# A gate table spread by one-hot products: one comparison for both keys of eight tokens, and one multiplication by the gates

## The chip, the cores and the metric

The kernel runs on one core of a Trainium2 chip. The metric is the time of one execution on the device in microseconds (us). Engines are named as in the profile: PE is TensorE (PEld its weight loads), DVE is VectorE, ACT is ScalarE, POOL is GpSimd, SP is SyncE, which here only issues transfers.

## The reference

One decoder layer over 1024 tokens of width 1024: two kinds of attention, an output projection, and a mixture of 16384 single-neuron experts that are addressed by product keys. The change lies in the mixture:

```python
vals, idx = lax.top_k(sc, PEER_TOPK)          # per token and head: the best 16 of 128 keys, twice
cand = vals[:, :, 0, :, None] + vals[:, :, 1, None, :]
best, flat = lax.top_k(cand.reshape(..., 256), PEER_TOPK)
i1 = jnp.take_along_axis(idx[:, :, 0], flat // PEER_TOPK, axis=-1)
i2 = jnp.take_along_axis(idx[:, :, 1], flat % PEER_TOPK, axis=-1)
expert = i1 * PEER_NKEYS + i2                 # 8 heads x 16 = 128 experts for each token
gate = jax.nn.softmax(best, axis=-1)
act = jax.nn.gelu(jnp.einsum('td,thkd->thk', tc, u_emb[expert]))
out = jnp.einsum('thk,thkd->td', act * gate, v_emb[expert])
```

## The kernel before

The kernel is a sequence of stages on one core: projections, two attentions, the output projection, `route` (which finds 128 experts and gates for each token), `spread_gates`, and `run_experts`. The first 384 tokens (SPT = 3 tiles of 128) get their experts by gathering rows. For the other 640 tokens (NDT = 5 tiles, TD = 640) the kernel computes with all 16384 experts, and needs the gate of each token and expert in a dense table, which is zero where an expert wasn't chosen. `spread_gates` makes this table and writes it to `core.scr_g` in device memory, from where `run_experts` reads it.

`route` leaves `slotT` in SBUF, f32: for slot s (on the partitions, 128 of them) and token t it holds the first key, the second key and the gate. In `spread_gates` the view `flat` has these as planes 0, 1 and 2. A token's 128x128 table is a product of two factors with the slots as the summed dimension: `first[s, i]` is the gate if the first key is i, else 0; `second[s, j]` is 1 if the second key is j, else 0.

The work goes in octets of 8 tokens (OCT = 8, NOCT = 80 octets, 16 octets to a tile), with two buffers (BUFS = 2) for the factors and four pairs of PSUM banks (PS_BUFS = 4). Each engine runs its own loop, ordered by semaphores:

- DVE (L1676 to L1686) compares a bf16 iota with the second keys of the octet (L1676, 1024 elements for each partition, written as [key, token] to `one2`), then makes `first` in 8 operations, one for each token (L1683: iota equal to the first key, times the gate, f32), and then converts the last 2 of the octet's 8 second factors to f32 and turns them from [key, token] to [token, key] order (L1686). It waits on `second_act`, `second_dve` and `spread_done` for free buffers, and on `ones_ready` in front of L1686.
- ACT (L1708) converts and turns the other 6 (ON_ACT = 6) second factors (`widen`), and copies each finished octet from PSUM to `gates` in SBUF (L1716, `copy_out`). The order is widen(n+1), copy_out(n).
- PE (L1699) waits for all three parts and for a free pair of banks, and does one f32 product for each token, `first[:, b, t, :]` as the stationary operand (weights) and `second[:, b, t, :]` as the moving one. The profile counts two weight loads and two matmuls for one such product, so 16 of each for an octet.
- SP (L1652) sends each finished tile of `gates` (8 MB) to device memory; near the end it loads what the next stage needs first (L1655 to L1658), and after the last octet it sends the last tile in two parts (L1662).

In the trace `one` is the tile `one2`, `iota_g` is `iota_f`, `iota_gb` the bf16 `iota`, and `slot_keys` is `keysT`.

Of the kernel before, what the change touches and what calls it, by code (L numbers as in the profile page):

```python
# [6 lines left out]
P = 128  # L7
# [22 lines left out]
PH, NKEY, PQ, TOPK = 8, 128, 256, 16  # L30
# [8 lines left out]
TD = SEQ - T0  # L39
# [18 lines left out]
bf16 = mybir.dt.bfloat16  # L58
i32 = mybir.dt.int32
u32 = mybir.dt.uint32  # L60
ALU = mybir.AluOpType
# [39 lines left out]
def clear_counts(nc, sems):  # L101

    with nc.Block() as block:
        @block.sync
        def _(sp):
            for s in sems:
                sp.sem_clear(s)
# [1494 lines left out]
def spread_gates(core, slotT, outer, hn_in, u_in, last_sent):  # L1602

    nc, ps = core.nc, core.ps
    OCT = 8
    TU = BANK // NKEY
    NB = OCT // TU
    BUFS = 2
    PS_BUFS = 4
    PER_TILE = P // OCT  # L1610
    NOCT = TD // OCT
    ON_ACT = 6
    LEAD = 8
    with ExitStack() as ctx:
        sb, new_sem = core.scope(ctx)
        made = []

        def sem(name):
            made.append(new_sem(name))
            return made[-1]  # L1620

        with nc.sbuf_tensor("gates1", [P, NKEY, P], f32, side="right") as gates1:
            pass
        lead = Lead(core, outer)
        gates = [ctx.enter_context(nc.sbuf_tensor("gates0", [P, NKEY, P], f32, side="right")), gates1]
        one2 = sb("one2", [P, BUFS, NKEY, OCT], bf16)
        first = sb("first", [P, BUFS, OCT, NKEY])
        second = sb("second", [P, BUFS, OCT, NKEY])
        iota_f = sb("iota_g", [P, NKEY])
        iota = sb("iota_gb", [P, NKEY, OCT], bf16)  # L1630
        keysT = sb("slot_keys", [P, TD], bf16)
        iota_in = sem("iota_in_g")
        iota_ready, keys_ready = sem("iota_ready_g"), sem("keys_ready_g")
        ones_ready, first_ready, second_act, second_dve = (sem(x) for x in (
            "ones_ready", "first_ready", "second_act", "second_dve"))
        spread_done, gates_out = sem("spread_done"), sem("gates_out")
        sent = [sem(f"gates_sent{k}") for k in range(2)]
        clear_counts(nc, (*made, hn_in, *u_in, *last_sent))
        block = ctx.enter_context(nc.Block())
        flat = slotT[:, :, :, :].rearrange("p z i t -> p z (i t)")  # L1640

        def need(eng, sem_, value):
            if value > 0:
                eng.wait_ge(sem_, value)

        @block.sync
        def _(sp):
            sp.dma_start(iota_f[:, :], core.i["c_iota"]).then_inc(iota_in, 16)
            dst = core.scr_g.rearrange("j i t -> i j t")
            for tile in range(NDT - 1):  # L1650
                sp.wait_ge(gates_out, (tile + 1) * PER_TILE)
                sp.dma_start(dst[:, :, tile * P:(tile + 1) * P], gates[tile % 2][:, :, :]).then_inc(sent[tile % 2], 16)  # L1652
            assert NDT % 2 == 1
            sp.wait_ge(sent[1], 16 * (NDT // 2))
            sp.dma_start(lead.u_raw[:, 0, :], core.i["uT"][0]).then_inc(u_in[0], 16)  # L1655
            sp.dma_start(lead.hn_hi[:, :, :].bitcast(f32), core.scr_hi).then_inc(hn_in, 16)
            sp.dma_start(lead.hn_lo[:, :, :].bitcast(f32), core.scr_lo).then_inc(hn_in, 16)
            sp.dma_start(lead.u_raw[:, 1, :], core.i["uT"][1]).then_inc(u_in[1], 16)  # L1658
            sp.wait_ge(sent[0], 16 * (NDT // 2))
            sp.wait_ge(gates_out, NDT * PER_TILE)  # L1660
            for part, js in enumerate((slice(0, LEAD), slice(LEAD, NKEY))):
                sp.dma_start(dst[:, js, (NDT - 1) * P:], gates[0][:, js, :]).then_inc(last_sent[part], 16)  # L1662

        @block.vector
        def _(dve):
            dve.wait_ge(iota_in, 16)
            nc.vector.tensor_copy(iota[:, :, :], iota_f[:, :].rearrange("p (i o) -> p i o", o=1)
                                  .to_broadcast([P, NKEY, OCT])).then_inc(iota_ready, 1)
            nc.vector.tensor_copy(keysT[:, :], flat[:, 1, :]).then_inc(keys_ready, 1)
            dve.wait_ge(iota_ready, 1)  # L1670
            dve.wait_ge(keys_ready, 1)
            for n in range(NOCT):
                b = n % BUFS
                need(dve, second_act, n - BUFS + 1)
                need(dve, second_dve, n - BUFS + 1)
                nc.vector.tensor_tensor(  # L1676
                    one2[:, b, :, :], iota[:, :, :],
                    keysT[:, n * OCT:(n + 1) * OCT].rearrange("p (o t) -> p o t", o=1)
                    .to_broadcast([P, NKEY, OCT]), ALU.is_equal).then_inc(ones_ready, 1)
                need(dve, spread_done, n - BUFS + 1)  # L1680
                for t in range(OCT):
                    at = n * OCT + t
                    nc.vector.tensor_scalar(first[:, b, t, :], iota_f[:, :], flat[:, 0, at:at + 1], flat[:, 2, at:at + 1],  # L1683
                                            ALU.is_equal, ALU.mult).then_inc(first_ready, 1)
                dve.wait_ge(ones_ready, n + 1)
                nc.vector.tensor_copy(second[:, b, ON_ACT:, :], one2[:, b, :, ON_ACT:].rearrange("p i t -> p t i")  # L1686
                                      ).then_inc(second_dve, 1)

        @block.tensor
        def _(pe):  # L1690
            for n in range(NOCT):
                b, bank = n % BUFS, NB * (n % PS_BUFS)
                pe.wait_ge(first_ready, (n + 1) * OCT)
                pe.wait_ge(second_act, n + 1)
                pe.wait_ge(second_dve, n + 1)
                need(pe, gates_out, n - PS_BUFS + 1)
                for t in range(OCT):
                    slot = ps[:, bank + t // TU, :].rearrange("p (i t) -> p t i", t=TU)[:, t % TU, :]
                    last = nc.tensor.matmul(slot, first[:, b, t, :], second[:, b, t, :], start=True, stop=True)  # L1699
                last.then_inc(spread_done, 1)  # L1700

        @block.scalar
        def _(act):
            def widen(n):
                b = n % BUFS
                act.wait_ge(ones_ready, n + 1)
                need(act, spread_done, n - BUFS + 1)
                nc.scalar.activation(second[:, b, 0:ON_ACT, :], one2[:, b, :, 0:ON_ACT].rearrange("p i t -> p t i"),  # L1708
                                     ACT.Copy).then_inc(second_act, 1)

            def copy_out(n):
                tile, q, bank = n // PER_TILE, n % PER_TILE, NB * (n % PS_BUFS)
                if q == 0:
                    need(act, sent[tile % 2], 16 * (tile // 2))
                act.wait_ge(spread_done, n + 1)
                nc.scalar.activation(  # L1716
                    gates[tile % 2][:, :, q * OCT:(q + 1) * OCT].rearrange("p j (u t) -> p j u t", u=NB),
                    ps[:, bank:bank + NB, :].rearrange("p u (j t) -> p j u t", t=TU), ACT.Copy).then_inc(gates_out, 1)

            widen(0)  # L1720
            for n in range(NOCT):
                if n + 1 < NOCT:
                    widen(n + 1)
                copy_out(n)
    return lead
# [608 lines left out]
```

## Time and profile before

| what | value |
|---|---|
| median of 3 runs | 3493.8 us (3491.78 to 3494.56) |
| the profiled execution | 3491.57 us, of which the span of the trace is 3489.8 us |
| mean granted PE clock | 0.966 of 2.4 GHz |
| stage of the change (`spread_gates`) | about 1299 to 1540 us of the span |

A row of the grouped views reads: line, engine, operation, tile written and tiles read, shape (partitions x elements for each partition), count, then busy time and the mean duration of one in ns, and then the idle time of the engine just before these instructions and what ended it. In the timeline the first number is the start in us and the second the time from the start of the first to the end of the last instruction of the row. Instructions of one engine overlap a little, so the distance between two starts is less than a duration.

### The profile page before, as it was taken

How to read it: one execution, taken by the hardware profiler on the slowest of the kernel's cores; microseconds unless marked ns; L12 is line 12 of the kernel's file. 1: busy time of each engine (PE TensorE's matmuls, PEld its weight loads, DVE VectorE, ACT ScalarE, POOL GpSimd, SP SyncE). 2: the span in 40 equal slices, each digit the busy share in tenths (PEclk: the TensorE clock that was granted, in tenths of full speed). 3: DMA queues.
4: the chain of work that ended last, by engine and by line, in shares of the span. 5: the costliest groups of instructions: out<-in, count | busy, mean ns of one | idle time of the engine just before them, and what ended most of it. 6: DMA issues, size and time to landing. Idle time of an engine off the chain costs nothing.

```text
span 3489.8 us, 48281 instructions
## 1 busy us (share of the span) xinstructions
PE 3149.8 (90%) x17341; PEld 2488.5 (71%) x17341; DVE 2190.4 (63%) x5408; ACT 1066.5 (31%) x1515; POOL 980.6 (28%) x943
## 2 busy tenths in 40 slices
PE   8997888997999936659999999999999999999997
PEld 4445666744887826658889877887788888788885
DVE  2112333323598979967888877777677777544544
ACT  2224545511333319962222222222122222222221
POOL 0000000000122220003333356566566656322222
PEclk9998889998999969999999999999999999999998
DMA  5213102112111103688777789999999999765765
GB/s 192 81 64 108 30 6 49 24 43 80 67 63 61 53 5 97 193 265 290 258 259 256 253 323 363 359 378 370 344 373 382 364 359 376 263 248 218 255 232 197
DMA packets 319597, 715.63 MB, mean 205 GB/s; under 512 B 48816, under 2 KB 154544, under 8 KB 318000
## 3 DMA queue, kind: packets, MB, share of 16 engines
q0 software_dynamic: 110592, 402.70, 31.4%
q1 hardware_dynamic: 201792, 299.95, 24.6%
q10 hardware_dynamic: 7024, 10.51, 0.8%
q8 instruction: 112, 1.84, 0.2%
q14 instruction: 77, 0.63, 0.1%
HBM read 633.91 MB, written 75.50 MB: 203 GB/s over the span
## 4 chain that ended last, share of the span: by engine, by line
PE 50%; DVE 3%; DMA 2%; issue 1%; ACT 0%; POOL 0%; POOLq 0%; ACTq 0%; DVEq 0%
PE psum L1965 23%; PE psum L1949 22%; PE psum L1992 5%; DMA w<-scr_g 1%; DVE res L2139 1%; DVE res L2128 1%; DMA res<-u_rows,eid 0%; DVE u_lo L2096 0%; DMA rows<-scr_rows 0%; DVE w_lo L2113 0%; DMA v_ring<-v_rows,eidT 0%; POOL v_ring L1933 0%; DVE v_lo L2118 0%; ACT u_hi L2027 0%; DVE w L2104 0%
## 5 line engine op out<-in xcount | busy, mean ns | idle before, releaser
L1933 POOL DMA_INDIRECT v_ring<-v_rows,eidT x384 | 443.2, 1154 | 622.3 <-PE psum L1992 513.8
L1949 PE MATMUL psum<-hn_hi_e,u_hi 128*128 128x320 f32 x1792 | 557.7, 311 | 27.4 <-DVE w L2108 18.9
L1949 PE MATMUL psum<-hn_lo_e,u_hi 128*128 128x320 f32 x1792 | 557.0, 311 | 0.0
L1949 PE MATMUL psum<-hn_hi_e,u_lo 128*128 128x320 f32 x1792 | 556.1, 310 | 0.0
L1965 PE MATMUL psum<-v_hi,w_hi 128*128 128x512 f32 x1280 | 511.5, 400 | 21.7 <-DVE res L2128 11.0
L2128 DVE TENSOR_TENSOR res<-psum,res 128x512 f32<-128x512 f32 x640 | 431.9, 686 | 122.8 <-PE psum L1965 122.4
L1965 PE MATMUL psum<-v_hi,w_lo 128*128 128x512 f32 x1280 | 501.0, 391 | 0.0
L1965 PE MATMUL psum<-v_lo,w_hi 128*128 128x512 f32 x1280 | 500.9, 391 | 0.0
L1926 POOL DMA_INDIRECT res<-u_rows,eid x288 | 337.7, 1173 | 336.8 <-DVE dots L2139 277.7
L2139 DVE CUSTOM_DVE_ANT_0 res<-res,rows 128x1024 f32<-128x1024 f32 x288 | 349.4, 1218 | 56.4 <-DMA res<-u_rows,eid 45.8
L2033 ACT ACTIVATE psum<-psum 128x640 f32<-128x640 f32 x112 | 77.1, 688 | 938.5 <-PE psum L1949 938.5
L1949 PEld LDWEIGHTS psum<-hn_hi_e,u_hi 128*128 128x128 f32 x1792 | 339.4, 189 | 32.4 <-issue 28.0
L1965 PEld LDWEIGHTS psum<-v_hi,w_hi 128*128 128x128 f32 x1280 | 241.1, 188 | 148.4 <-issue 78.3
L1949 PEld LDWEIGHTS psum<-hn_lo_e,u_hi 128*128 128x128 f32 x1792 | 339.3, 189 | 4.5
L1949 PEld LDWEIGHTS psum<-hn_hi_e,u_lo 128*128 128x128 f32 x1792 | 339.3, 189 | 0.0
L2108 DVE TENSOR_TENSOR w<-psum,w 128x640 f32<-128x640 f32 x112 | 92.3, 824 | 366.1 <-ACT psum L2033 341.9
L1965 PEld LDWEIGHTS psum<-v_hi,w_lo 128*128 128x128 f32 x1280 | 241.4, 189 | 51.4
L1965 PEld LDWEIGHTS psum<-v_lo,w_hi 128*128 128x128 f32 x1280 | 241.4, 189 | 46.4
L1699 PE MATMUL psum<-second,first 128*128 128x128 f32 x1280 | 164.0, 282 | 79.9 <-DVE second L1686 79.7
L2044 ACT ACTIVATE v_hi<-v_raw 128x1024 fp32r<-128x1024 f32 x128 | 128.4, 1051 | 330.8 <-PE psum L1965 330.8
L1699 PEld LDWEIGHTS psum<-second,first 128*128 128x128 f32 x1280 | 151.3, 194 | 92.7 <-DVE first L1683 92.3
L469 PE MATMUL psum<-w_in,hT 128*128 128x512 f32 (+1 forms) x512 | 211.3, 575 | 0.0
(242 smaller groups left out, 4648.3 us busy)
## 6 DMA issues: line engine op xcount, KB each, us to landing
v_raw<-v_rows SPq DMA_DIRECT2D x128, 512.0 KB, 6.7
u_raw<-uT SPq DMA_DIRECT2D x112, 512.0 KB, 6.4
w<-scr_g SPq DMA_DIRECT2D x128, 320.0 KB, 4.5
scr_g<-gates SPq DMA_DIRECT2D x4, 8192.0 KB, 30.7
scr_m<-st_m SPq DMA_DIRECT2D x8, 1024.0 KB, 4.0
w_raw<-in_w_pq SPq DMA_DIRECT2D x8, 1024.0 KB, 7.4
u_raw_r<-uT SPq DMA_DIRECT2D x16, 512.0 KB, 3.5
scr_g<-gates SPq DMA_DIRECT2D x1, 7680.0 KB, 30.9
```

The source lines that it names most:

```text
L469: last = nc.tensor.matmul(ps[:, 2 + c, 0:width(c)], hT[:, k, j, :], w_in[:, j, c * BANK:c * BANK + width(c)], start=j == 0, stop=j == KD - 1)
L1699: last = nc.tensor.matmul(slot, first[:, b, t, :], second[:, b, t, :], start=True, stop=True)
L1926: pool.indirect_dma_start(u_slot(n % U_RING), None, core.i["u_rows"], bass.IndirectOffsetOnAxis(eid[:, n // P, n % P:n % P + 1], 0)).then_ ...
L1933: pool.indirect_dma_start(v_ring[:, m % V_RING, :], None, core.i["v_rows"], bass.IndirectOffsetOnAxis(eidT[:, m // P, t:t + 1], 0)).then_i ...
L1949: last = nc.tensor.matmul(ps[:, a, 0:COLS], x[:, c, j, :], y[:, j, a * COLS:(a + 1) * COLS], start=m == 0, stop=m == len(terms) - 1)
L1965: last = nc.tensor.matmul(ps[:, OUT_AT + F % OUT_BANKS, :], x[:, b, c, i * P:(i + 1) * P], y[:, c, half * BANK:(half + 1) * BANK], start=m ...
L1992: last = nc.tensor.matmul(ps[k * QUAD:(k + 1) * QUAD, SUM_AT + half, :], strip[:, p % 2, at:at + QUAD], v_ring[:, n % V_RING, half * BANK: ...
L2033: nc.scalar.activation(ps[:, 0:ACTS, 0:COLS], ps[:, 0:ACTS, 0:COLS], ACT.Gelu).then_inc(gelu_ready, 1)
L2044: nc.scalar.activation(v_hi[:, c, :], v_raw[:, c, :], ACT.Copy).then_inc(v_hi_ready, 1)
L2108: nc.vector.tensor_tensor(half, ps[:, 0:ACTS, 0:COLS], half, ALU.mult).then_inc(w_ready, 1)
L2128: nc.vector.tensor_tensor(r, ps[:, OUT_AT + F % OUT_BANKS, :], r, ALU.add).then_inc(added, 1)
L2139: nc.vector.tensor_tensor_reduce(out=x, in0=x, in1=rows[:, :], scale=1.0, scalar=0.0, op0=ALU.mult, op1=ALU.add, accum_out=dots[:, tile % ...
```

## The change

The comparison is made once for both keys of an octet (2048 elements for each partition instead of 1024); `one2` becomes `ones` with a plane for each key, and `keysT` holds both keys in bf16. `first` is then one multiplication of the first plane by the gates (1024 elements), in place of 8 operations. It is written in the order of the comparison, [key, token], so that the weights of token t are now `first[:, b, :, t]`: 128 elements of 4 bytes, each 32 bytes from the last. Before, they were 128 neighbouring elements. The wait on `ones_ready` now stands in front of this multiplication. Nothing else of the stage is changed: the second factors, the products, the copies and the transfers are the same in number and size.

```diff
-        one2 = sb("one2", [P, BUFS, NKEY, OCT], bf16)
-        first = sb("first", [P, BUFS, OCT, NKEY])
+        ones = sb("ones", [P, BUFS, 2, NKEY, OCT], bf16)
+        first = sb("first", [P, BUFS, NKEY, OCT])
-        keysT = sb("slot_keys", [P, TD], bf16)
+        keysT = sb("slot_keys", [P, 2, TD], bf16)
@@ vector
-            nc.vector.tensor_copy(keysT[:, :], flat[:, 1, :]).then_inc(keys_ready, 1)
+            nc.vector.tensor_copy(keysT[:, :, :], flat[:, 0:2, :]).then_inc(keys_ready, 1)
                 nc.vector.tensor_tensor(
-                    one2[:, b, :, :], iota[:, :, :],
-                    keysT[:, n * OCT:(n + 1) * OCT].rearrange("p (o t) -> p o t", o=1)
-                    .to_broadcast([P, NKEY, OCT]), ALU.is_equal).then_inc(ones_ready, 1)
+                    ones[:, b, :, :, :],
+                    iota[:, :, :].rearrange("p (o i) t -> p o i t", o=1).to_broadcast([P, 2, NKEY, OCT]),
+                    keysT[:, :, n * OCT:(n + 1) * OCT].rearrange("p z (o t) -> p z o t", o=1)
+                    .to_broadcast([P, 2, NKEY, OCT]), ALU.is_equal).then_inc(ones_ready, 1)
                 need(dve, spread_done, n - BUFS + 1)
-                for t in range(OCT):
-                    at = n * OCT + t
-                    nc.vector.tensor_scalar(first[:, b, t, :], iota_f[:, :], flat[:, 0, at:at + 1], flat[:, 2, at:at + 1],
-                                            ALU.is_equal, ALU.mult).then_inc(first_ready, 1)
                 dve.wait_ge(ones_ready, n + 1)
-                nc.vector.tensor_copy(second[:, b, ON_ACT:, :], one2[:, b, :, ON_ACT:].rearrange("p i t -> p t i")
+                nc.vector.tensor_tensor(
+                    first[:, b, :, :], ones[:, b, 0, :, :],
+                    flat[:, 2, n * OCT:(n + 1) * OCT].rearrange("p (o t) -> p o t", o=1).to_broadcast([P, NKEY, OCT]),
+                    ALU.mult).then_inc(first_ready, 1)
+                nc.vector.tensor_copy(second[:, b, ON_ACT:, :], ones[:, b, 1, :, ON_ACT:].rearrange("p i t -> p t i")
                                       ).then_inc(second_dve, 1)
@@ tensor
-                pe.wait_ge(first_ready, (n + 1) * OCT)
+                pe.wait_ge(first_ready, n + 1)
-                    last = nc.tensor.matmul(slot, first[:, b, t, :], second[:, b, t, :], start=True, stop=True)
+                    last = nc.tensor.matmul(slot, first[:, b, :, t], second[:, b, t, :], start=True, stop=True)
@@ scalar
-                nc.scalar.activation(second[:, b, 0:ON_ACT, :], one2[:, b, :, 0:ON_ACT].rearrange("p i t -> p t i"),
+                nc.scalar.activation(second[:, b, 0:ON_ACT, :], ones[:, b, 1, :, 0:ON_ACT].rearrange("p i t -> p t i"),
```

## Rows read from the trace of the kernel before

**Rows 1.** All instructions of L1676: durations min/median/max, first and last start.

```profile
L1676 DVE TENSOR_TENSOR one<-iota_gb,slot_keys x80: 672/694/707, 1299.8 to 1533.4; 128x1024 bf16<-128x1024 bf16 x80
```

**Rows 2.** Groups of the stage, 1303 to 1530 us.

```profile
L1699 PE MATMUL psum<-second,first 128*128 128x128 f32 x1232 | 157.9, 282 | 77.1 <-DVE second L1686 76.9 <-ACT second L1708 0.2
L1699 PEld LDWEIGHTS psum<-second,first 128*128 128x128 f32 x1232 | 145.7, 194 | 89.4 <-DVE first L1683 89.0 <-issue 0.3
L1708 ACT ACTIVATE second<-one 128x768 f32<-128x768 bf16 x77 | 125.4, 1629 | 19.3 <-DVE one L1676 19.2
L1716 ACT ACTIVATE gates<-psum 128x1024 f32<-128x1024 f32 x77 | 78.9, 1025 | 5.8 <-PE psum L1699 1.7
...
L1686 DVE CAST second<-one 128x256 f32<-128x256 bf16 x76 | 29.6, 390 | 0.0
```

**Rows 3.** Timeline of one octet's period, from 1380 us.

```profile
1379.92 0.68 DVE L1676 TENSOR_TENSOR one<-iota_gb,slot_keys 128x1024 bf16<-128x1024 bf16 x1
1380.22 1.86 PEld L1699 LDWEIGHTS psum<-second,first 128*128 128x128 f32 x16 [1.09 <-DVE first L1683]
1380.26 2.02 PE L1699 MATMUL psum<-second,first 128*128 128x128 f32 x16 [0.93 <-DVE second L1686]
1380.52 2.13 DVE L1683 TENSOR_SCALAR first<-iota_g,slotT 128x128 f32<-128x128 f32 x8
1380.63 1.63 ACT L1708 ACTIVATE second<-one 128x768 f32<-128x768 bf16 x1 [0.24 <-DVE one L1676]
1382.31 1.02 ACT L1716 ACTIVATE gates<-psum 128x1024 f32<-128x1024 f32 x1
1382.57 0.38 DVE L1686 CAST second<-one 128x256 f32<-128x256 bf16 x1
1382.87 0.68 DVE L1676 TENSOR_TENSOR one<-iota_gb,slot_keys 128x1024 bf16<-128x1024 bf16 x1
...
1383.58 1.65 ACT L1708 ACTIVATE second<-one 128x768 f32<-128x768 bf16 x1 [0.24 <-DVE one L1676]
```

**Rows 4.** Busy time in one tile's stretch of the stage, with granted clock.

```profile
1394.00:1441.00 47.00, 32.13 (x256) 29.66 (x256) 47.00 (x160) 42.28 (x33) 0.00 (x0) 1.00 0.63 180
```

**Rows 5.** End of the stage: timeline, and the chain that ended last.

```profile
1538.77 1.02 ACT L1716 ACTIVATE gates<-psum 128x1024 f32<-128x1024 f32 x1 [1.93 <-PE psum L1699]
1539.88 0.99 SPq L1662 DMA_DIRECT2D scr_g<-gates  x2
...
1544.68 27.36 DMA w<-scr_g
```

**Rows 6.** Transfers of the stage: count, KB each, median us to landing.

```profile
scr_g<-gates SPq DMA_DIRECT2D x4, 8192.0 KB, 30.7
```

**Rows 7.** L1499, bf16 comparisons around 1272 us, durations min/median/max.

```profile
L1499 DVE TENSOR_TENSOR hit<-at,iota_p x2: 491/738/984, 1271.5 to 1271.9; 128x640 bf16<-128x640 bf16 x1, 128x1600 bf16<-128x1600 bf16 x1
```

**Rows 8.** Groups of the whole span, shapes kept apart.

```profile
L2118 DVE TENSOR_TENSOR v_lo<-v_raw,v_hi 128x1024 fp32r<-128x1024 f32 x128 | 150.7, 1218 | 6.5 <-ACT v_hi L2044 6.5
```

**Rows 9.** Timeline of DVE: an instruction that waits for the one before it.

```profile
1275.17 0.27 DVE L1529 TENSOR_REDUCE den_p<-ex 128x8 f32<-128x128 f32 x1
1275.48 0.20 DVE L1530 RECIPROCAL den_p<-den_p 128x8 f32<-128x8 f32 x1
```

**Rows 10.** Groups of 1295 to 1560 us: the conversion of the keys.

```profile
L1669 DVE CAST slot_keys<-slotT 128x640 bf16<-128x640 f32 x1 | 0.5, 485 | 0.0
```

**Rows 11.** Groups of the whole span: three reductions on DVE.

```profile
L1522 DVE TENSOR_REDUCE expert<-found 128x32 f32<-128x416 f32 x16 | 14.9, 930 | 0.0
L1518 DVE TENSOR_REDUCE expert<-found 128x32 f32<-128x320 f32 x16 | 12.1, 756 | 0.0
...
L1529 DVE TENSOR_REDUCE den_p<-ex 128x8 f32<-128x128 f32 x8 | 2.3, 285 | 15.1 <-ACT ex L1391 15.1
```

**Rows 12.** All instructions of L2044 and of L1320: durations min/median/max.

```profile
L2044 ACT ACTIVATE v_hi<-v_raw x128: 1037/1044/1067, 1584.7 to 3442.9; 128x1024 fp32r<-128x1024 f32 x128
L1320 PE MATMUL psum<-keysT,peer_qT x256: 272/275/348, 890.3 to 1231.0; 128*128 128x128 f32 x128
```

## The prediction

> **What bounds the kernel now.** The change touches one stage, so the first question is where that stage lies and what sets its pace. All instructions of L1676, one per octet, give both [rows 1]: 80 of them, the first at 1299.8 us and the last at 1533.4, so an octet takes 233.6 / 79 = 2.957 us. The timeline of one octet shows the same, 2.95 us from one comparison to the next [rows 3]. In it DVE has no gap: the comparison takes 0.60 us to the next start, the eight operations 2.05, the conversion 0.30, sum 2.95. In one tile's stretch DVE is busy for 47.00 of 47.00 us, at a granted PE clock of 1.00, that is 2.4 GHz [rows 4]. The other engines wait for it. PE works 2.02 us of an octet and then sits idle 0.93 us for DVE; its loads show 1.09 [rows 2, 3]. ACT waits only 0.24 us for the comparison [rows 3], so it is nearly full: from the widening's start to the copy's 1.68 us, and 1.03 more until the copy ends, 2.71 us an octet.
>
> Then, does the stage count for the end? After its last copy (1538.77 + 1.02 us) SP sends the last tile, and the next stage hangs on a read of `scr_g` behind it [rows 5]. None of that can start before the last octet, so what an octet gains or loses goes 80-fold into the end. The tile transfers do not bound: 30.7 us each [rows 6] against 16 octets, 47.3 us now.
>
> **The change part by part.**
>
> *DVE, comparison.* bf16 comparisons of 1024, 640 and 1600 elements took 694, 491 and 984 ns [rows 1, 7]. From 640 to 1600 that is 0.51 ns an element; the 1600 one has the same form of operands as the new one, each repeated along an outer index. So 2048 elements: 984 + 448 x 0.51 = 1.21 us. F32 operations take twice that: 1218 ns for 1024 elements and 285 for 128, (1218 - 285) / 896 = 1.04 ns [rows 8, 11]. If the larger pattern fell back to this, it would be 1.21 + 2048 x 0.52 = 2.28 us; nothing in these rows points to it.
>
> *DVE, multiplication.* It has an f32 operand and an f32 result, as L2118, whose 1024 elements took 1218 ns [rows 8]. The bound below is the 0.69 us of the all-bf16 comparison of as many elements [rows 1]. I take 1.22, since the gates and the result are f32.
>
> *DVE, order.* The multiplication must wait for the comparison just before it. In a pair of that kind the second began 0.04 us after the first's end (1275.17 + 0.27, then 1275.48) [rows 9]. Other neighbours overlap by 0.08 to 0.09 us [rows 3]. Behind the waiting instruction stand the conversion L1686, for which PE waits, and the next comparison, for which ACT waits. Octet on DVE: 1.21 + 0.04 + (1.22 - 0.09) + 0.30 = **2.68 us**, against 2.95.
>
> *ACT.* Its work stays at 2.71 us an octet; the comparison is ready 0.5 us later in its own octet, but ACT's loop doesn't wait twice, so this shifts its phase and takes nothing from its pace. With DVE at 2.68, ACT becomes the slowest of the two, 2.71 to 2.74 with hand-overs. So on these engines alone the change could win 0.23 us an octet at best, although it removes 640 instructions.
>
> *PE, where I choose.* Weights of one token were 128 neighbouring f32; now each is 32 bytes from the last. No weight load in this trace reads with such a step, so its price has to be bounded. Below: as now. Sixteen loads lie within 1.86 us, the last one 0.19 long, so one starts each (1.86 - 0.19) / 15 = 0.111 us, 0.87 ns a column; the matmuls come each (2.02 - 0.275) / 15 = 0.116 us [rows 3]. Above: what a 32-byte step costs elsewhere. L1522 and L1518 sum f32 that lie 8 elements, 32 bytes, apart; L1529 sums neighbours: 285 ns for 128 elements, of which 128 x 1.04 = 133 is streaming and 152 fixed. The strided ones: (930 - 152) / 416 = 1.87 ns and (756 - 152) / 320 = 1.89 ns an element, not 1.04 [rows 11]. ACT's widening L1708 reads bf16 with a step of 16 bytes: 768 elements in 1629 ns; L2044 and L1716 read in runs, 1024 in 1044 and 1025 ns [rows 2, 12]. With 0.83 ns for each of theirs and 190 fixed, L1708 pays (1629 - 190) / 768 = 1.87 ns. L1686, on DVE with the same step, pays (390 - 152) / 256 = 0.93, the same 1.86 for each pair if it reads two at a time [rows 2]. Two engines with different paces, two types and two steps meet at one time, 1.87 ns. That looks like a limit of the memory, not of an engine, so I expect PE's loads to meet it too: 128 x 1.87 = 0.239 us a load. The loads now hide behind the matmul before them; longer than the 0.116 us of a matmul, they set the pace themselves. With 0 to 0.009 us between them, as now: 0.239 to 0.248 us, sixteen **3.83 to 3.97 us** an octet, above all other engines. I take 0.242, 3.87 us.
>
> What speaks against it is on PE's output side: the products of L1699 are written to PSUM 16 bytes apart and take 275 ns in the timeline, as those of L1320, which are written in a row (median 275) [rows 2, 3, 12]. PE may hide what others pay.
>
> The Trainium skill, "Advanced Engine Details and Errata", SBUF Cachelines, says that an access which moves on to another 16-byte line each time is slow, for any engine; it gives no figure. The reductions above agree with it. The same page, PSUM Cachelines, says the like of matmul outputs, and there this trace does not agree, by the 275 ns on both sides.
>
> *Buffers and transfers in that case.* While PE works on an octet for 3.87 us, DVE makes the next (2.7 us) and then waits for `spread_done`, ACT widens and copies (2.7 us) and waits as well; four pairs of banks keep PE from waiting for the copies. PE would run without gaps. A tile's octets then take 62 us, so its transfer has still more room.
>
> *Ends.* The keys' conversion doubles to 1280 elements: 640 took 485 ns [rows 10], so 0.33 us more, once. The first octet reaches PE about 0.3 us sooner. They cancel.
>
> **Sum.** 80 x (3.87 - 2.957) = +73 us. Against the profiled execution's own 3491.6 us that is 3564.6. The median of the runs stands 2.2 us above that execution, so I forecast **3567 us** for a median. Its own range: 80 x (3.83 - 2.957) = +70 to 80 x (3.97 - 2.957) = +81, so 3561 to 3575, a little wider, 3555 to 3580.
>
> **The rivals.**
>
> 1. *PE doesn't pay for the step* (the other side). Then ACT's 2.71 to 2.74 us bound the octet: 80 x (2.72 - 2.957) = -19 us, **3475 us**. For it: PSUM's 16-byte step costs nothing; no row shows a slow load. It decides by one number: an octet of loads shorter than 2.957 us means a pace under 0.185 us, 1.44 ns a column; below 0.17 us PE drops out of the sum. The Trainium skill, "TensorE: Matmul & The Clock Gate", LDWEIGHTS, gives a load's time by its columns alone, with no word of their step; by that rule this rival is the forecast, and for neighbouring columns the 0.111 us agree with it.
> 2. *The step only doubles a load*, 0.222 us: 3.55 us an octet, +48, about 3541 us. A weaker form of mine.
> 3. *The load no longer hides*: load and matmul follow each other, 0.242 + 0.116 = 0.358 us, 5.7 us an octet, +221, about 3715 us. Against it: loads run ahead of matmuls throughout [rows 3].
> 4. *The comparison falls to one element per cycle*: 2.28 us, DVE 3.75 an octet, +64 even if PE pays nothing, about 3557 us. The 984 ns of rows 7 speak against it.
> 5. *Nothing to measure*: a load pace of 0.180 to 0.190 us that happens to meet the old octet, or DVE's gain lost to more hand-overs.
>
> **How the numbers follow.** Chances: my forecast 0.50, rival 1 0.31, rival 2 0.08, rival 3 0.04, rival 4 0.02, rival 5 0.05. The predicted time is that of the likeliest, 3567. To leave out no more than 2 in 10 the range must reach rival 1: 3470 to 3580 us; it is wide because one unmeasured price decides the sign, and the likeliest case alone has 3555 to 3580. A measurement of this kernel tells 0.2% (7 us) from no change. Slower: 0.50 + 0.08 + 0.04 + 0.02 = 0.64; faster 0.31; same 0.05.
>
> **What the changed kernel's profile would show.** Right: the comparison at 1.21 us and the multiplication at 1.22, 0.04 us apart; in each octet sixteen loads over 3.8 us or more, one each 0.24 us, each lasting some 0.3 us; PE without idle time in the stage; DVE and ACT waiting for PE for about 1.2 us an octet; the stage from 1299 to about 1613 us; later stages unchanged. Wrong: loads still 0.11 us apart, PE waiting for ACT's widening, ACT without a gap and the stage over at about 1520 us. Also wrong would be a comparison of 2.3 us, or a granted clock below 1.00 in the stage because the matmuls stand further apart; at 1.2 GHz this trace shows nothing of a strided load, and that part of the price is open.

## The result, and the profile after

The changed kernel takes 3557.97 us in the median (3556.88 to 3559.22, 4 runs), beside 3494.18 us before (3491.78 to 3497.29, 4 runs). The medians differ by 63.8 us, 1.8%; the ratio is put at 1.0185, 95% interval 1.0173 to 1.0197, so the kernel is slower, clear of noise. The span of the profiled execution grew from 3489.8 to 3557.0 us, by 67.2.

First the pace of the stage. All instructions of L1676 and L1700 after the change (durations min/median/max in ns, first and last start in us):

```profile
L1676 DVE TENSOR_TENSOR ones<-iota_gb,slot_keys x80: 1214/1220/1229, 1301.3 to 1599.4; 128x2048 bf16<-128x2048 bf16 x80
L1700 PEld LDWEIGHTS psum<-second,first x1280: 312/335/340, 1304.2 to 1608.8; 128*128 128x128 f32 x183
L1700 PE MATMUL psum<-second,first x1280: 343/402/575, 1304.2 to 1608.9; 128*128 128x128 f32 x183
```

The comparisons now spread over 298.1 us instead of 233.6 [rows 1]; the first starts only 1.5 us later. A weight load lasts 335 ns, not 194; there are as many as before. The groups of the stage, 1303 to 1600 us, show who waits:

```profile
L1700 PEld LDWEIGHTS psum<-second,first 128*128 128x128 f32 x1243 | 296.1, 335 | 8.4 <-DVE first L1683 8.4
L1700 PE MATMUL psum<-second,first 128*128 128x128 f32 x1242 | 296.0, 402 | 8.2 <-ACT second L1709 8.2
L1709 ACT ACTIVATE second<-ones 128x768 f32<-128x768 bf16 x79 | 129.0, 1633 | 7.1 <-DVE ones L1676 7.1
L1683 DVE TENSOR_TENSOR first<-ones,slotT 128x1024 f32<-128x1024 bf16 x79 | 96.8, 1226 | 87.2 <-PE psum L1700 87.1
...
L1717 ACT ACTIVATE gates<-psum 128x1024 f32<-128x1024 f32 x77 | 78.9, 1024 | 96.9 <-PE psum L1700 96.9
```

PE has no idle time but the 8.2 us at the start, where 77 us stood in [rows 2]. It is VectorE that waits now, 87 us for PE, and ScalarE, 97 us. One octet in the timeline:

```profile
1379.70 8.43 PEld L1700 LDWEIGHTS psum<-second,first 128*128 128x128 f32 x35
...
1380.74 1.02 ACT L1717 ACTIVATE gates<-psum 128x1024 f32<-128x1024 f32 x1 [1.26 <-PE psum L1700]
1380.74 1.23 DVE L1683 TENSOR_TENSOR first<-ones,slotT 128x1024 f32<-128x1024 bf16 x1 [1.14 <-PE psum L1700]
1381.66 1.64 ACT L1709 ACTIVATE second<-ones 128x768 f32<-128x768 bf16 x1
1381.88 0.39 DVE L1687 CAST second<-ones 128x256 f32<-128x256 bf16 x1
1382.19 1.22 DVE L1676 TENSOR_TENSOR ones<-iota_gb,slot_keys 128x2048 bf16<-128x2048 bf16 x1
1384.55 1.02 ACT L1717 ACTIVATE gates<-psum 128x1024 f32<-128x1024 f32 x1 [1.25 <-PE psum L1700]
```

From one copy to the next it is 3.81 us (1384.55 - 1380.74), where [rows 3] has 2.95. The 35 loads in a row come each (8.43 - 0.335) / 34 = 0.238 us, where sixteen came 0.111 apart. The row by stretches, to be laid beside [rows 4], shows PE busy for the whole stretch, and the granted clock unchanged:

```profile
1394.00:1441.00 47.00, 47.00 (x199) 47.00 (x199) 32.88 (x37) 31.37 (x25) 0.00 (x0) 1.00 0.33 93
```

The end of the stage, answering to [rows 5]:

```profile
1609.34 1.02 ACT L1717 ACTIVATE gates<-psum 128x1024 f32<-128x1024 f32 x1 [2.79 <-PE psum L1700]
1610.44 1.00 SPq L1662 DMA_DIRECT2D scr_g<-gates  x2
```

The last copy starts at 1609.34 us instead of 1538.77, 70.6 later. In this execution 1.2 of it was there before the stage (the bf16 iota is made at 1299.76 us, before at 1298.55), so the stage costs 69.4 us. The span grew by 67.2: the stages behind gave back 3.4 us. That is within what two executions of one kernel differ by (the four runs of the kernel before spread over 5.5 us).

### The profile page after: what moved, and what is told of

Read it like the earlier page. It is cut to its first block, busy times and chain, and to the rows that moved or that the text cites. A ratio compares the mean times of both kernels' runs of the same rounds, so it can differ in the third digit from the quotient of the medians.

```text
span 3557.0 us, 47799 instructions
## 1 busy us (share of the span) xinstructions
PE 3289.5 (92%) x17341; PEld 2640.0 (74%) x17341; DVE 2168.1 (61%) x4848; ACT 1059.2 (30%) x1515; POOL 981.2 (28%) x943
## 3 DMA queue, kind: packets, MB, share of 16 engines
q8 instruction: 111, 1.82, 0.2%
## 4 chain that ended last, share of the span: by engine, by line
PE 49%; DVE 2%; DMA 2%; issue 1%; ACT 0%; POOL 0%; POOLq 0%; ACTq 0%; DVEq 0%
PE psum L1966 23%; PE psum L1950 22%; PE psum L1993 5%; DMA w<-scr_g 1%; DVE res L2140 1%; DVE res L2129 1%; DVE u_lo L2097 0%; DMA rows<-scr_rows 0%; DVE w_lo L2114 0%; DMA v_ring<-v_rows,eidT 0%; POOL v_ring L1934 0%; DMA res<-u_rows,eid 0%; DVE v_lo L2119 0%; ACT u_hi L2028 0%; DVE w L2105 0%
## 5 line engine op out<-in xcount | busy, mean ns | idle before, releaser
L1700 PE MATMUL psum<-second,first 128*128 128x128 f32 x1280 | 305.1, 402 | 8.2 <-ACT second L1709 8.2
L1700 PEld LDWEIGHTS psum<-second,first 128*128 128x128 f32 x1280 | 304.9, 335 | 8.4 <-DVE first L1683 8.4
```

The source lines that it names most:

```text
L1700: last = nc.tensor.matmul(slot, first[:, b, :, t], second[:, b, t, :], start=True, stop=True)
```

## The experiments

In these kernels only the layout of a factor, or the engine that makes it, differs. Diffs are against the changed kernel unless said otherwise, and `...` marks what a line leaves out. A time without a number of runs is that of a single run. The kernel before ran beside them: 3493.16 us in the median beside experiments 1 to 4 (3484.29 to 3497.47, 11 runs), 3497.40 us beside 5 to 8 (3491.30 to 3499.66, 7 runs). A single time can so stand 6 to 9 us off its median, and the argument rests on the pace inside the stage.

**1. The step alone.** This is the kernel before, with nothing but the layout of `first` changed:

```diff
-        first = sb("first", [P, BUFS, OCT, NKEY])
+        first = sb("first", [P, BUFS, NKEY, OCT])
-                    nc.vector.tensor_scalar(first[:, b, t, :], iota_f[:, :], ...
+                    nc.vector.tensor_scalar(first[:, b, :, t], iota_f[:, :], ...
-                    last = nc.tensor.matmul(slot, first[:, b, t, :], second[:, b, t, :], start=True, stop=True)
+                    last = nc.tensor.matmul(slot, first[:, b, :, t], second[:, b, t, :], start=True, stop=True)
```

> The kernel before with one thing changed: its eight small operations still make the first factors, but write each token's 128 values 32 bytes apart, and PE reads its weights with that step. The result is the same. Theory A (the step of the weight reads is the whole cost): PE alone sets the pace, one weight load each 0.238 us as in the changed kernel, 3.81 us an octet, so about 3558 us, although VectorE's work is the old one (2.95 us, or a little more if its strided writes are slower). Rival B (the loss comes from the two wide VectorE operations, their order or their traffic): the loads stay 0.111 us apart, the octet takes 2.95 us and the time is that of before, 3494 us.

Measured: 3555.87 us, 2 us from the changed kernel and 62.7 above the kernel before beside it. The groups of 1310 to 1500 us:

```profile
L1699 PE MATMUL psum<-second,first 128*128 128x128 f32 x800 | 190.7, 402 | 0.0
L1699 PEld LDWEIGHTS psum<-second,first 128*128 128x128 f32 x799 | 190.4, 335 | 0.0
L1683 DVE TENSOR_SCALAR first<-iota_g,slotT 128x128 f32<-128x128 f32 x400 | 110.4, 404 | 37.7 <-PE psum L1699 37.7
```

Loads of 335 ns again and PE without idle time, with the eight small operations still in place. The step explains the loss, and VectorE's new form adds nothing to it. (The small operations, which now write 32 bytes apart, grew as well, mean 404 ns from 348, but VectorE has time: it waits for PE.)

**2. A step of 16 bytes.** Two groups of four tokens:

```diff
-        first = sb("first", [P, BUFS, NKEY, OCT])
+        first = sb("first", [P, BUFS, OCT // 4, NKEY, 4])
-                    first[:, b, :, :], ones[:, b, 0, :, :],
-                    flat[:, 2, ...].rearrange("p (o t) -> p o t", o=1).to_broadcast([P, NKEY, OCT]),
+                    first[:, b, :, :, :], ones[:, b, 0, :, :].rearrange("p i (g t) -> p g i t", t=4),
+                    flat[:, 2, ...].rearrange("p (g o t) -> p g o t", o=1, t=4).to_broadcast([P, OCT // 4, NKEY, 4]),
-... matmul(slot, first[:, b, :, t], ...
+... matmul(slot, first[:, b, t // 4, :, t % 4], ...
```

> The changed kernel, but the product with the gates is written as two groups of four tokens, so that one token's weights are 16 bytes apart instead of 32. The result is the same. Theory A in the form that each access which finds a new 16-byte stretch costs 1.86 ns (ScalarE's bf16 reads 16 bytes apart paid that): the loads stay 0.238 us apart and the time about 3558 us. Rival B (VectorE's order or traffic): also 3558 us. Rival C (the cost grows with the distance, or the limit lies at more than 16 bytes): the loads come nearer to 0.111 us, and at 2.72 us an octet the time is about 3475 us.

Measured: 3545.71 us; the octet takes 3.73 us (copies start at 1399.99 and 1403.72), a load 0.233. In the groups of 1310 to 1500 us:

```profile
L1700 PEld LDWEIGHTS psum<-second,first 128*128 128x128 f32 x816 | 190.5, 330 | 0.0
L1709 ACT ACTIVATE second<-ones 128x768 f32<-128x768 bf16 x51 | 82.1, 1610 | 0.0
```

So 16 bytes cost nearly what 32 do. Distance itself has only a small part in it. Of the 12 us below the expected 3558, the shorter octets make 80 x (3.81 - 3.73) = 6.4, and 5.3 lay before the stage (the first comparison is at 1296.0 us instead of 1301.3).

**3. A step of 8 bytes.** The same edit with groups of two tokens (`OCT // 2`, `t // 2`, `t % 2`).

> The changed kernel, but the product with the gates is written as four groups of two tokens, so that one token's weights are 8 bytes apart: two of them lie in each 16-byte stretch. The result is the same. Theory A: a load pays 1.86 ns for every second column only, 0.93 ns a column, 0.119 us a load, 1.9 us an octet, so PE is no longer the bound; VectorE takes 2.68 us and ScalarE 2.71, and the time is 19 us under that of before, about 3475 us. If any step but the unbroken one halves the rate of the loads, they stay 0.238 us apart and the time is 3558 us. Rival B (the wide VectorE operations themselves): 3558 us. If VectorE's own reads in groups of two bf16 are slowed to 1.86 ns, its multiplication takes 2.05 us and the time is about 3536 us.

Measured: 3476.92 us in the median of 8 runs (3474.68 to 3482.97), ratio to before 0.9958, interval 0.9947 to 0.9969. This kernel is called kernel 3 below. One octet of its timeline:

```profile
1399.98 1.22 DVE L1676 TENSOR_TENSOR ones<-iota_gb,slot_keys 128x2048 bf16<-128x2048 bf16 x1
1400.00 1.00 ACT L1717 ACTIVATE gates<-psum 128x1024 f32<-128x1024 f32 x1
1400.30 1.96 PEld L1700 LDWEIGHTS psum<-second,first 128*128 128x128 f32 x16 [0.80 <-DVE first L1683]
1400.33 2.12 PE L1700 MATMUL psum<-second,first 128*128 128x128 f32 x16 [0.64 <-ACT second L1709]
1401.24 1.63 ACT L1709 ACTIVATE second<-ones 128x768 f32<-128x768 bf16 x1 [0.23 <-DVE ones L1676]
1401.31 1.23 DVE L1683 TENSOR_TENSOR first<-ones,slotT 128x1024 f32<-128x1024 bf16 x1
1402.45 0.38 DVE L1687 CAST second<-ones 128x256 f32<-128x256 bf16 x1
1402.74 1.22 DVE L1676 TENSOR_TENSOR ones<-iota_gb,slot_keys 128x2048 bf16<-128x2048 bf16 x1
```

The loads come each (1.96 - 0.196) / 15 = 0.118 us, 0.92 ns a column, half of the 1.86. PE waits again, and the octet takes 2.76 us. So the wide operations do gain, 16 us in the medians (3493.16 before), when PE can read their result at nearly its old pace. VectorE is still the one without time: 2.76 instead of 2.68, since the multiplication starts 0.11 us after the comparison's end (1401.31 against 1399.98 + 1.22), not 0.04.

**4. The old layout, written with a step.** The multiplication turns its result while writing it:

```diff
-        first = sb("first", [P, BUFS, NKEY, OCT])
+        first = sb("first", [P, BUFS, OCT, NKEY])
-                    first[:, b, :, :], ones[:, b, 0, :, :],
+                    first[:, b, :, :].rearrange("p t i -> p i t"), ones[:, b, 0, :, :],
-... matmul(slot, first[:, b, :, t], ...
+... matmul(slot, first[:, b, t, :], ...
```

> The changed kernel, but the multiplication writes its result in the old order, the 128 weights of a token side by side, by writing each element 512 bytes from the last. The result is the same. Theory A: PE's loads are back at 0.111 us apart. If VectorE's writes with a large step are free, the multiplication stays at 1.22 us and the time is about 3475 us, set by ScalarE; if each write with a step costs 1.87 ns as the reads do, it takes 2.07 us, the VectorE octet 3.53 us and the time is about 3540 us, now bound by VectorE. Rival B (the wide operations' order or traffic, not the layout): the loads stay 0.238 us apart and the time 3558 us.

Measured: 3529.73 us. The groups of 1310 to 1500 us:

```profile
L1683 DVE TENSOR_TENSOR first<-ones,slotT 128x1024 f32<-128x1024 bf16 x57 | 112.5, 1974 | 5.9
L1700 PEld LDWEIGHTS psum<-second,first 128*128 128x128 f32 x897 | 105.2, 193 | 85.2 <-DVE first L1683 85.2
```

The loads are back at 193 ns: it was the layout that PE reads, not VectorE's traffic. But a write of each element into a new place costs too, 1974 ns instead of 1226 for 1024 elements, 0.73 ns more for each, 1.77 in all with the 1.04 of before. That is a little under the 2.07 us expected for a price of 1.87 ns. The price only moved from PE to VectorE, whose octet is now 3.42 us (L1676 at 1399.12 and 1402.54).

**5. The step on the moving side.** Kernel 3, and `second` is not turned: 32 bytes between a token's moving elements.

```diff
-        second = sb("second", [P, BUFS, OCT, NKEY])
+        second = sb("second", [P, BUFS, NKEY, OCT])
-                nc.vector.tensor_copy(second[:, b, ON_ACT:, :], ones[:, b, 1, :, ON_ACT:].rearrange("p i t -> p t i")
+                nc.vector.tensor_copy(second[:, b, :, ON_ACT:], ones[:, b, 1, :, ON_ACT:]
-... matmul(slot, ..., second[:, b, t, :], ...
+... matmul(slot, ..., second[:, b, :, t], ...
-                nc.scalar.activation(second[:, b, 0:ON_ACT, :], ones[:, b, 1, :, 0:ON_ACT].rearrange("p i t -> p t i"),
+                nc.scalar.activation(second[:, b, :, 0:ON_ACT], ones[:, b, 1, :, 0:ON_ACT],
```

> The kernel with first factors 8 bytes apart (3477 us), but the second factors are no longer turned: each token's 128 moving elements lie 32 bytes apart, and ScalarE and VectorE convert them without a turn. The result is the same. If a step costs PE's moving reads what it costs its weight reads (1.86 ns a column), the matmuls come each 0.238 us, the octet takes 3.81 us and the time is about 3558 us, although ScalarE's widening falls from 1.63 to about 0.83 us. If only weight reads pay, VectorE's 2.68 us bound the octet and the time is about 3472 us.

Measured: 3561.47 us. The groups of 1310 to 1490 us:

```profile
L1700 PE MATMUL psum<-second,first 128*128 128x128 f32 x770 | 180.8, 414 | 0.0
L1700 PEld LDWEIGHTS psum<-second,first 128*128 128x128 f32 x769 | 165.9, 217 | 14.5
...
L1709 ACT ACTIVATE second<-ones 128x768 f32<-128x768 bf16 x48 | 42.0, 875 | 0.0
```

Here the loads stay near their old length (217 ns) and the matmuls, 414 ns long, come each 180.8 / 770 = 0.235 us. The moving operand pays the same price. The turn in ScalarE's widening, 1.63 us instead of 0.88, was what the kernel before paid to spare PE this.

**6. Both sides.** The changed kernel with the edit of experiment 5: 32 bytes on both operands.

> The changed kernel, but the second factors are not turned either: weights and moving elements both lie 32 bytes apart. The result is the same. If PE reads weights and moving elements side by side, and each pays for its own step, the pace stays 0.238 us and the time 3558 us. If the two reads share what the step uses up, a weight load and a matmul take 0.476 us together, the octet 7.6 us and the time is about 3865 us. If moving reads don't pay, 3558 us as well, so this is read with the run in which only the moving elements are stepped.

Measured: 3565.04 us. In the groups of 1310 to 1490 us the matmuls come each 180.6 / 753 = 0.240 us:

```profile
L1700 PE MATMUL psum<-second,first 128*128 128x128 f32 x753 | 180.6, 420 | 0.0
L1700 PEld LDWEIGHTS psum<-second,first 128*128 128x128 f32 x753 | 180.5, 337 | 0.0
```

Not 0.476: the two reads run side by side, and the pace with both steps is within 1% of that with a step on the weights alone (0.238).

**7. Eight bytes on both sides.** Kernel 3, with `second` in groups of two as well.

```diff
-        second = sb("second", [P, BUFS, OCT, NKEY])
+        second = sb("second", [P, BUFS, OCT // 2, NKEY, 2])
-                nc.vector.tensor_copy(second[:, b, ON_ACT:, :], ones[:, b, 1, :, ON_ACT:].rearrange("p i t -> p t i")
+                nc.vector.tensor_copy(second[:, b, ON_ACT // 2:, :, :], ones[:, b, 1, :, ON_ACT:].rearrange("p i (g t) -> p g i t", t=2)
-... ones[:, b, 1, :, 0:ON_ACT].rearrange("p i t -> p t i"),
+... ones[:, b, 1, :, 0:ON_ACT].rearrange("p i (g t) -> p g i t", t=2),
-... matmul(slot, ..., second[:, b, t, :], ...
+... matmul(slot, ..., second[:, b, t // 2, :, t % 2], ...
```

> Both factors as groups of two tokens, 8 bytes between the elements of a token, also for the second factors. The result is the same. ScalarE's widening then reads runs of two bf16 and should pay 0.93 ns an element or less, about 0.9 us instead of 1.63. If PE takes an 8-byte step on both sides at 0.12 us, VectorE becomes the bound with 2.68 us an octet and the time is 22 us under before, about 3471 us. If the two 8-byte steps together slow PE (0.17 us or more), it is 3475 us or more.

Measured: 3478.14 us, which as a whole is not told apart from kernel 3. ScalarE's widening fell to 932 ns as expected, but its time was not the bound. VectorE's octet is 2.67 us (comparisons at 1399.63 and 1402.30), 0.09 less than in kernel 3, and its 80 comparisons start within 210.6 us (1303.7 to 1514.3) instead of 218.3 (1300.6 to 1518.9). These 7.7 us don't reach the end in this one execution: some 3 were lost before the stage, and the rest behind it.

**8. ScalarE makes all of `second`.** Experiment 7 with ON_ACT = 8; VectorE's conversion is left out, and its wait for a free buffer stands on its own multiplication.

```diff
-    ON_ACT = 6
+    ON_ACT = 8
-                need(dve, second_dve, n - BUFS + 1)
+                need(dve, first_ready, n - BUFS + 1)
-                nc.vector.tensor_copy(second[:, b, ON_ACT:, :], ...).then_inc(second_dve, 1)
-                pe.wait_ge(second_dve, n + 1)
```

> As the run before it, but ScalarE converts all eight second factors, so VectorE has only the comparison and the multiplication left. The result is the same. VectorE: 1.21 + 0.04 + 1.13 = 2.38 us an octet. ScalarE: about 1.14 + 1.01 = 2.2 us. PE: 16 x 0.12 = 1.9 us. So about 2.4 us an octet, 80 x (2.4 - 2.957) = -45 us, about 3450 us. If the wide VectorE operations were slower beside ScalarE's reads, or PE slower with both steps (0.15 us or more), it would be about 3470 us.

Measured: 3455.98 us in the median of 4 runs (3455.11 to 3460.42), ratio to before 0.9887, interval 0.9871 to 0.9904. In the timeline:

```profile
1400.90 1.22 DVE L1676 TENSOR_TENSOR ones<-iota_gb,slot_keys 128x2048 bf16<-128x2048 bf16 x1
1401.04 1.96 PEld L1697 LDWEIGHTS psum<-second,first 128*128 128x128 f32 x16 [0.51 <-DVE first L1683]
1401.04 2.15 PE L1697 MATMUL psum<-second,first 128*128 128x128 f32 x16 [0.31 <-DVE first L1683]
1402.15 1.15 ACT L1706 ACTIVATE second<-ones 128x1024 f32<-128x1024 bf16 x1 [0.36 <-DVE ones L1676]
1402.22 1.23 DVE L1683 TENSOR_TENSOR first<-ones,slotT 128x1024 f32<-128x1024 bf16 x1
1403.23 1.02 ACT L1714 ACTIVATE gates<-psum 128x1024 f32<-128x1024 f32 x1
1403.37 1.22 DVE L1676 TENSOR_TENSOR ones<-iota_gb,slot_keys 128x2048 bf16<-128x2048 bf16 x1
```

2.47 us an octet (1403.37 - 1400.90), still VectorE's. The expected 2.38 had 0.04 us between the comparison's end and the multiplication; it is 0.10 (1402.22 against 1400.90 + 1.22). This is the fastest kernel here, 41 us under the one before, and it keeps the change's wide operations.

Not all that the stage gains arrives at its end. The chain that ended last has, between the send of the last tile and the next stage's work:

```profile
1502.91 11.06 DMA scr_g<-gates
1513.99 26.79 DMA w<-scr_g
```

From the issue of that send to the read of `scr_g` it is 11.1 us, where the kernel before needs 4.8 (1539.88 to 1544.68 in [rows 5]) and the changed one 4.8 (1610.44 to 1615.24). In kernel 3 it is 8.0 (1525.23 to 1533.20), in the kernel of experiment 7 8.3. The first part of the last tile, 512 KB, landed after 11.1, 8.0 and 8.3 us, and after 3.4 in the two slower kernels. In these three kernels it is sent while the loads for the next stage (L1655 to L1658) are still landing: here `hn_lo_e`, issued at 1495.10 us, needed 15.5. In the kernel before it had been issued at 1524.40 us and needed 15.1, so it was through. That these loads cause the delay fits all five traces, but was not tried apart.

## Why the prediction was right

- *VectorE bounds the stage before, and all of it counts for the end*: right. Where VectorE's octet got shorter and PE's did not get in the way (experiments 3 and 8), the time fell. With the change an octet grew by 0.86 us, the stage by 69.4 and the span by 67.2.
- *The comparison keeps its pace, the multiplication takes that of f32*: 1.220 us for twice 1024 elements, where one 1024 took 0.694, so (1220 - 694) / 1024 = 0.51 ns for each element more; the multiplication 1.226. Forecast were 1.21 and 1.22. Rival 4 is out by this, and by VectorE's 87 us of waiting for PE; the time alone could not have told, for its 3557 us would have met the measured one as well. The 984 ns that the forecast started from was a lucky pick: [rows 7] shows two of the instructions of L1499, but the sixteen of 1600 elements in that trace have a mean of 1532 ns and reach 2082, and the prediction gave no reason for taking the short one.
- *The order on VectorE*: 0.04 us between the two in the first octet; in later ones, where a wait on `spread_done` stands before it as well, 0.11 (experiment 3); that this second wait is the reason was not tried apart. The term of 2.68 us was too small by 0.08 (experiment 3). It didn't matter in the changed kernel, whose VectorE waits.
- *PE's weights*: the term that decides. Forecast 0.242 us a load (0.239 to 0.248), measured 0.238, just under that range, which is 1.86 ns a column: the price of 1.87 read off VectorE's reductions and ScalarE's widening holds for PE to a hundredth. Experiments 1 and 4 show that it is the layout of the weights and nothing else in the change. That the three engines meet one limit of the memory, as the prediction argues, is not shown; the equal prices fit it. Rival 1 is what remains when the step is made harmless (experiment 3): forecast 3475 us, measured 3477. That agreement is in part luck, for the bound was VectorE at 2.76 us, not ScalarE, and 3.2 us were lost behind the stage. Rival 2's 0.222 us and rival 3's 0.358 are out.
- *The size*: 3567 forecast, 3558 measured. The sum had +73 us; with the measured pace it is 80 x (3.81 - 2.957) = +68, since the loads came each 0.238 us and I had taken 0.242. The stage itself shows +69.4, the whole span +67.2, the medians +63.8. So about half of the miss is that one term, and the other half is no more than what separates one execution from another.
- *The argument against it* was PE's output, written 16 bytes apart at no cost. That row was true and said nothing of PE's reads.
- The Trainium skill, "Advanced Engine Details and Errata", SBUF Cachelines, gives the 16-byte line as the unit, and two hits on a line as what it takes to hide the latency, without naming an engine; experiments 2 and 3 agree for PE's weights: 0.233 us a load at 16 bytes, 0.118 at 8.
- The Trainium skill, "TensorE: Matmul & The Clock Gate", LDWEIGHTS, has a load's time depend on the number of columns alone; these runs disagree, 0.111 us against 0.238 for the same 128 columns at a granted clock of 1.00.

The prediction left open what a step costs at 1.2 GHz, and the traces answer it. Both kernels begin the stage at the lower level: from 1304.50 to 1307.50 us the granted clock is 0.50 in each. The loads of that window, first in the kernel before, then in the changed one:

```profile
1304.36 3.32 PEld L1699 LDWEIGHTS psum<-second,first 128*128 128x128 f32 x15
1304.21 3.42 PEld L1700 LDWEIGHTS psum<-second,first 128*128 128x128 f32 x14 [8.38 <-DVE first L1683]
```

A load lasts 0.333 us in the first row and 0.336 in the second, so they come each (3.32 - 0.333) / 14 = 0.213 us side by side and (3.42 - 0.336) / 13 = 0.237 at 32 bytes. The stepped load takes at 1.2 GHz what it takes at 2.4 (0.238), and only the load without a step is slower, 0.213 instead of 0.111. So the step costs 0.127 us a load at 2.4 GHz and 0.024 at 1.2.

Not settled: why 32 bytes cost 2% more than 16 (0.238 against 0.233).

## What to carry to other kernels

A step that saves the writer of an operand work must be priced on its reader too. Here the price could be read off other engines that already made such a read in the trace; it had to be confirmed by a run. Layouts are not all or nothing: groups of two f32 kept most of a wide operation's simple form and nearly all of PE's pace. When one engine is made faster, list what every other engine of the loop needs for the same item; here PE had 0.93 us an octet to spare and its work grew by 1.8. And when a stage gets shorter, look at what its transfers then meet: the fastest kernel gave 6 us back behind the stage.

## What the runs showed of the hardware

- At 2.4 GHz PE reads f32 weights at 0.87 ns a column when they are side by side, 0.92 with 8 bytes between starts, 1.82 with 16 and 1.86 with 32. At 1.2 GHz it is 1.67 side by side and 1.85 with 32. The moving operand at 32 bytes: 0.235 us for 128 columns in each of a product's two matmuls.
- With a step on both operands the pace is nearly that of one, 0.240 us: that is 1% above the weights' own 0.238 and 2% above the moving operand's own 0.235.
- VectorE's f32 writes 512 bytes apart took 1974 ns for 1024 elements, beside 1226 in a row, 0.73 ns more for each element; the f32 reads 32 bytes apart in [rows 11] paid 0.83 to 0.85 more. Writes 32 bytes apart (experiment 1) took 404 ns for 128 elements instead of 348, 0.44 more for each. PE's writes to PSUM 16 bytes apart paid next to nothing: its matmuls come each 0.116 us in the kernel before, those of L1320, which write in a row, each 0.112 (sixteen in 1.95 us, the last 0.275 long).
- ScalarE read bf16 in pairs, 4 of every 16 bytes, in 932 ns for 768 elements, beside 875 in runs of six (written in runs of six, too) and 1633 one at a time.
